# Where a V projection is cut: two strips by depth, or two strips by columns

## The reference

```python
ATT_PATTERNS = ((128, 1), (512, 4), (2048, 16))      # window, dilation of the three groups
h = rms_norm(x, norm1_w) * (1.0 + sc1) + sh1         # 512 tokens x 1024
proj = h @ w_in                                      # att_in = the first 3 * 3 * 512 columns
qkv = att_in.reshape(b, s, 3, 3, 8, 64)              # group, (q, k, v), head, 64 channels
for g, (window, dilation) in enumerate(ATT_PATTERNS):
    o, l = dilated_window_attention(qkv[:, :, g, 0], qkv[:, :, g, 1], qkv[:, :, g, 2], window, dilation)
wts = softmax(stack(lses), axis=0)                   # the groups are mixed by their log sums
out = sum(wts[..., None] * stack(outs), axis=0)
```

## Time and profile before

| What | Value |
|---|---|
| Median of three launches | 2623.5 us (2619.78 to 2627.65) |
| The profiled launch | 2619.78 us, span 2618.1 us |
| TensorE matmul (PE) busy | 2374.2 us, 91% of the span |
| TensorE weight load (PEld) busy | 1901.7 us, 73% |
| VectorE (DVE) busy | 1339.6 us, 51% |
| GpSimd (POOL) busy | 1203.2 us, 46% |
| ScalarE (ACT) busy | 591.3 us, 23% |
| DMA share over the span | 22.2% on the main queue |

### The profile page before, as it was taken

How to read it: one execution, slowest core, us unless ns; L and a number is a source line. 1 busy time by engine, 2 the same in 40 slices (tenths; PEclk the granted TensorE clock), 3 DMA queues, 4 the chain that set the end, 5 groups by cost and what they waited for, 6 DMA issues and landing times.

```text
span 2618.1 us, 33224 instructions
## 1 busy us (share of the span) xinstructions
PE 2374.2 (91%) x12076; PEld 1901.7 (73%) x12076; DVE 1339.6 (51%) x1726; ACT 591.3 (23%) x1270; POOL 1203.2 (46%) x986
## 2 busy tenths in 40 slices
PE   5999887998988979999979999999998898989698
PEld 4887766865555757788858887887887676877586
DVE  7788235056655150200274555555555446888612
ACT  2000012132333011211222233223332212222101
POOL 4777645567676646153232112211211365665463
PEclk8999988988898989989989999999999998999899
DMA  3233223232333322021221011111102232222121
GB/s 108 89 97 97 80 64 95 75 106 89 115 96 99 103 65 81 29 85 41 68 68 42 29 50 49 29 35 44 35 1 90 65 129 80 96 80 80 60 88 60
DMA packets 220958, 189.31 MB, mean 72 GB/s; under 512 B 7837, under 2 KB 210220, under 8 KB 220588
## 3 DMA queue, kind: packets, MB, share of 16 engines
q1 hardware_dynamic: 212944, 181.81, 22.2%
q10 hardware_dynamic: 7900, 5.94, 0.8%
HBM read 179.30 MB, written 8.44 MB: 72 GB/s over the span
## 4 chain that ended last, share of the span: by engine, by line
PE 58%; DVE 16%; issue 8%; POOLq 8%; DVEq 4%; POOL 4%; DMA 1%; ACT 1%; ACTq 0%; SPq 0%
PE bank L730 9%; PE bank L731 8%; PE bank L732 8%; PE bank L1138 8%; POOLq L588 5%; POOL wlo L579 3%; DVEq L2214 2%; PE bank L964 2%; DVE hf L2223 1%; POOLq L578 1%; PE bank L1033 1%; PE bank L1035 1%; PE bank L1034 1%; PE bank L1017 1%; PE bank L1019 1%
## 5 line engine op out<-in xcount | busy, mean ns | idle before, releaser
L579 POOL TENSOR_TENSOR wlo<-raw,whi 128x1024 fp32r<-128x1024 f32 (+5 forms) x316 | 697.6, 2208 | 46.7 <-issue 5.9
L577 POOL TENSOR_SCALAR whi<-raw 128x1024 fp32r<-128x1024 f32 (+5 forms) x316 | 322.4, 1020 | 563.6 <-PE bank L1035 312.3
L553 POOL TENSOR_TENSOR spare<-ones 1x1 f32<-1x1 f32 x176 | 57.4, 326 | 745.7 <-PE bank L732 468.9
L730 PE MATMUL bank<-hbuf,whi 128*128 128x512 f32 (+2 forms) x904 | 357.1, 395 | 6.9 <-POOL wlo L579 6.9
L732 PE MATMUL bank<-hbuf,wlo 128*128 128x512 f32 (+2 forms) x904 | 353.9, 392 | 0.0
L731 PE MATMUL bank<-hbuf,whi 128*128 128x512 f32 (+1 forms) x776 | 302.7, 390 | 0.0
L730 PEld LDWEIGHTS bank<-hbuf,whi 128*128 128x128 f32 (+2 forms) x904 | 170.0, 188 | 46.1 <-POOL wlo L579 7.6
L732 PEld LDWEIGHTS bank<-hbuf,wlo 128*128 128x128 f32 (+2 forms) x904 | 169.6, 188 | 38.1
L731 PEld LDWEIGHTS bank<-hbuf,whi 128*128 128x128 f32 (+1 forms) x776 | 145.3, 187 | 32.2 <-issue 1.0
L1947 DVE TENSOR_REDUCE nmax<-bank 128x4 f32<-128x512 f32 (+3 forms) x40 | 21.6, 557 | 263.2 <-PE bank L966 263.2
L2143 DVE TENSOR_TENSOR hf<-bank,hf 128x512 f32<-128x512 f32 (+1 forms) x96 | 53.6, 558 | 158.1 <-PE bank L1138 156.6
(11 more groups left out here) (469 smaller groups left out, 5535.1 us busy)
## 6 DMA issues: line engine op xcount, KB each, us to landing
raw<-in_w_up SPq DMA_DIRECT2D x22, 1024.0 KB, 5.1
raw<-in_w_in SPq DMA_DIRECT2D x41, 512.0 KB, 4.0
raw<-in_w_in SPq DMA_DIRECT2D x18, 1024.0 KB, 5.1
raw<-in_pool_w_in SPq DMA_DIRECT2D x16, 1024.0 KB, 5.5
adaw<-in_w_ada SPq DMA_DIRECT2D x32, 512.0 KB, 3.8
raw<-in_mla_w_in SPq DMA_DIRECT2D x10, 1024.0 KB, 5.4
raw<-in_pool_w_out SPq DMA_DIRECT2D x8, 1024.0 KB, 5.2
raw<-in_w_ada SPq DMA_DIRECT2D x16, 512.0 KB, 3.9
```

What stands on the lines that cost most here:

```text
L577: G.tensor_scalar(h_, r_, 1.0, 1.0, ALU.mult, ALU.mult)
L579: G.tensor_tensor(l_, r_, f32(h_), ALU.subtract).then_inc(raw_split, 1)
L730: M.matmul(dst, wh, acts[k][0], start=(first and k == 0), stop=False)
```

## The change

The V weights of a group are cut by output columns and no longer by depth. Strip 4 now holds all eight depth tiles of output columns 0 to 255, strip 5 those of columns 256 to 511. That is the shape that the Q and K strips have, so the three groups of six strips become nine runs of two strips in the tables that SP and POOL follow. A PSUM bank now holds two token blocks of 256 columns each: bank 0 the blocks 0 and 1 and bank 1 the blocks 2 and 3 of the first column half, banks 2 and 3 the same of the second. A matmul has 256 moving columns, and there are 192 of them in a group's V product where there were 96. PE waits for both halves of a strip before it starts on it, and ACT takes each bank with two copies as before, with another access pattern, bank by bank as it is finished.

```diff
-          ("att", 3, 6), ("lora", 1, 2), ("rkv", PAIRS, 3), ("mix", 4, 2), ("wo", 2, 2), ("up", 11, 2),
+          ("att", 9, 2), ("lora", 1, 2), ("rkv", PAIRS, 3), ("mix", 4, 2), ("wo", 2, 2), ("up", 11, 2),
...
-                if j < 4:
-                    return w_in2[:, :, ds(i * 1536 + j * 256, 256)], 8, 256
-                return w_in2[:, (j - 4) * 4:(j - 3) * 4, ds(i * 1536 + 1024, 512)], 4, 512
+                return w_in2[:, :, ds(i * 512 + j * 256, 256)], 8, 256
...
                 for j in range(2):
-                    for blk in range(4):
-                        if j == 0:
-                            bank_free("att", blk, 3 * g + 2)
-                        for k in range(4):
-                            if blk == 0 and k in (0, 2):
-                                strip_ready(sg + 4 + j, k // 2)
-                            tokens = slice(blk * P, (blk + 1) * P) if g == 0 else slice(blk, S, 4)
-                            ah, al = [x[:, tokens] for x in h_out[j * 4 + k]]
-                            wh, wl = whi[j][:, k * S:(k + 1) * S], wlo[j][:, k * S:(k + 1) * S]
-                            M.matmul(bank[blk][:, :], ah, wh, start=(j == 0 and k == 0), stop=False)
-                            M.matmul(bank[blk][:, :], ah, wl, start=False, stop=False)
-                            mm = M.matmul(bank[blk][:, :], al, wh, start=False, stop=(j == 1 and k == 3))
-                        if blk % 2 == 1:
-                            mm.then_inc(products_done, 1)
+                    strip_ready(sg + 4 + j, 1)
+                    for hv in range(2):
+                        b = j * 2 + hv
+                        bank_free("att", b, 3 * g + 2)
+                        for t in range(2):
+                            blk = hv * 2 + t
+                            dst = bank[b][:, t * 256:(t + 1) * 256]
+                            for k in range(DT):
+                                if g == 0:
+                                    ah, al = [x[:, blk * P:(blk + 1) * P] for x in h_out[k]]
+                                else:
+                                    ah, al = [x[:, blk:S:4] for x in h_out[k]]
+                                wh, wl = whi[j][:, k * 256:(k + 1) * 256], wlo[j][:, k * 256:(k + 1) * 256]
+                                M.matmul(dst, ah, wh, start=(k == 0), stop=False)
+                                M.matmul(dst, ah, wl, start=False, stop=False)
+                                mm = M.matmul(dst, al, wh, start=False, stop=(k == DT - 1))
+                        mm.then_inc(products_done, 1)
...
-                for b in range(4):
-                    product_ready(sg + 5, b // 2)
-                    x = bank[b][:, :].rearrange("p (r par e) -> p r par e", r=4, par=2)
-                    for par in range(2):
-                        cp = A.copy(av6[:, b, :, par, par, :], x[:, :, par, :])
-                    cp.then_inc(evac[b], 1)
+                for j in range(2):
+                    for hv in range(2):
+                        b = j * 2 + hv
+                        product_ready(sg + 4 + j, hv)
+                        x = bank[b][:, :].rearrange("p (k r par e) -> p k r par e", k=2, r=2, par=2)
+                        for par in range(2):
+                            cp = A.copy(av6[:, 2 * hv:2 * hv + 2, 2 * j:2 * j + 2, par, par, :], x[:, :, :, par, :])
+                        cp.then_inc(evac[b], 1)
```

## The result

The changed kernel takes 2665.49 us (median of four launches, 2660.28 to 2669.54) where the kernel before takes 2624.53 us beside it. The ratio is 1.0156, with a 95% interval of 1.0133 to 1.0181: slower, by 35 to 47.5 us. The forecast was 2666 us. The launch that the profiler recorded is not among the four; it took 2673.77 us.

What follows compares the result with a forecast made beforehand. PE was taken as the bound, with V on the path at full length. +1.0 + 44.9 - 1.8 = +44.1 us on 2619.78 gave 2663.9, or 2667.6 by the median; forecast 2666 us, range 2652 to 2682.

Steps and rivals of the forecast that it cites:

- The step that carried it: V products of groups 1 and 2: stepped weight loads set a pace of 0.2351 us per matmul, +44.9 us.
- rival A: V of groups 1 and 2: stepped loads hide under the matmuls, total 2619.5 to 2622.6 us; chance 0.07.
- The subtraction that gave 0.232: Stepped V load of 310 ns less 81 ns fixed part leaves 229, plus 3 ns: 0.232 us pace.
- Group 0: V product of group 0, loads without a step: 256-column matmuls at a pace of 0.1187 us, +1.0 us.
- ACT's tail: Behind each V product: two copies left instead of four, 0.6 us less per group, -1.8 us in all.
- The whole-strip wait and the nine runs: V strips on PE, SP and POOL: hidden by POOL's idle time of 3.59 us per strip, cost 0.
- Rival B: Clock falls to 1.2 GHz inside V: 2736 us if for all of both products, 2700 for half; chance 0.06.
- Clock luck: Low-clock stretches behind V may come out shorter or longer with any shift; some 5 us either way.

Runs made afterwards that it cites:

- after_step23: The changed kernel with V's stationary tile read at a step of 2 values in group 1 and 3 in group 2; one launch, 2647.47 us.
- after_halves: The changed kernel with the wait for a V strip split into two halves again; one launch, 2666.31 us.
- after_nostep: The changed kernel with groups 1 and 2 reading V tokens in blocks of 128 neighbours, without the step; ratio 0.9974 to the kernel before.
- after_128: The changed kernel with group 1's V matmuls streaming only 128 of their 256 columns; one launch, 2690.74 us.
- before_nostep: The kernel before with the step taken out of V's token reads in groups 1 and 2, 512 columns kept; ratio 1.0017.
- after_64: The changed kernel with V matmuls of groups 0 and 1 streaming only 64 of their 256 columns; one launch, 2693.77 us.

## Why the prediction was right, point by point

**The step that carried it** was the upper bound for the stepped pace, 0.2351 us, taken because 229 + 3 = 0.232 lay beside it. Measured 0.2327. +44.9 us were forecast for the two groups' V; the trace gives 44.45 + 0.39 - 22.73 = 22.1 us each, +44.2. The lower bound (rival A) needed loads that hide, and after_step23 shows at which step they do: 2, not 4. The prediction read the old V products as bound by their loads already. Loads that bind have 0.2327 us, 2.4 ns under the old pace, so that was nearly so; what makes the 2.4 ns is open. The subtraction that gave 0.232 worked by luck in part. It fits loads that do not wait for each other; from the 329 ns of the changed kernel it would give 329 - 81 + 3 = 251 ns for a pace of 233, and from the 264 ns at a step of 3 it gives 186 for 175.

**Group 0**, +1.0 forecast: 22.91 + 0.28 - 21.92 = +1.3 measured. The pace is 0.1200 and not the 0.1187 of the MLA stream.

**ACT's tail**, -1.8 forecast: the gap from the last V matmul to the first score went from 1.88 to 1.22 us in group 0, from 2.00 to 1.47 in group 1, from 1.99 to 1.44 in group 2, 1.7 us in all. In groups 1 and 2 a tenth of a microsecond of that gap is the last matmul's own wait for its tile.

**The whole-strip wait and the nine runs**, 0 forecast: 0 by after_halves and by after_nostep.

**Rival B** came out as no event in the changed kernel (PEclk 1.00 in V). Its price does not fit: the factor of 1.80 was taken from line 988, which reads its tiles without a step, and after_128 shows 0.233 us at either level with 128 columns. A stream of 256 such columns at 1.2 GHz is in no trace. By an estimate of 1.80 x 0.120 = 0.216 us it would still hide under the load's 0.233, so by it V would have cost the same had the clock fallen, and only what stands behind V would have been slower. No run here tests that.

**Clock luck** was allowed with 5 us. Time at 0.50 within the profiled spans is 311 us before and 333 us after, of which 37.5 us stand in one stretch behind group 2. The price of a low stretch can now be read: from the first score to the last probabilities x V, groups 1 and 2 have the same number of instructions of the same shapes, and take 34.5 us with 10.2 us at 0.50 (the changed kernel, group 1), 37.4 with 17.1 (the kernel before, group 1), 41.9 with 27.3 (after_nostep, group 1), 44.8 with 34.1 (before_nostep, group 2) and 46.1 with 37.5. That is 0.42 us per us at the lower clock, near the 0.445 of the prediction's upper bound, so a single stretch can move a launch by 11.6 us. What sets its length stays open. The two kernels with thinner V streams had falls inside V (after_128, after_64), the others had none there.

**A term that may be missing** is the stretch behind group 0. The prediction named the shorter break only as luck. With the old gap of 1.88 us both profiled kernels (before, before_nostep) have a low stretch there, and the scores take 49.2 and 50.5 us. With a shorter gap eight of nine have none, after_step23 being the ninth, and the scores take 44.7 to 45.1 us; after_64, whose clock had fallen inside V, is left aside. If this holds beyond single traces, the change won some 4.5 us there, which would help to put the measured 41.0 us under the 43.9 of the V products. It was not tested.

## What to carry to other kernels

Two matmuls of half the width read the same columns but load twice as many stationary tiles, so look at the load's own pace before halving a width: take it from the start distances of a narrow stream. A load's duration less its fixed part gives it only as long as the loads do not wait for each other. If the stationary tile is read with a step, count the 16-byte lines it meets. And a wait put before the first instruction of a stage may belong before the first reader of what it waits for: that move won 1.1 to 1.7 us per group in the trace, where the regrouping of banks shortened the gap by 0.53 to 0.66.

## What the runs showed of the hardware

A weight load of 128 float32 columns costs 0.111 us of pace at 2.4 GHz and 0.213 us at 1.2 GHz without a step (after_64), and 0.233 us at either clock with a step of 16 bytes (the changed kernel, after_128, after_64). With a step of 12 bytes it is 0.1754 us and with 8 bytes not above 0.120 (after_step23, at 2.4 GHz). The two paces above 0.120 at that clock fit 1.82 ns per 16-byte line. Loads that bind stand back to back, and then the matmul's listed duration grows from 0.28 to 0.39 us with no idle time shown anywhere: PE reads as 100% busy in a stretch in which it gets through 256 columns every 0.233 us, though it takes 0.120 us for them in group 0. In the score stages of groups 1 and 2 each us at 1.2 GHz costs 0.42 us (five stretches of 10.2 to 37.5 us, in four traces).
